# Adding the residual inside the PSUM accumulator and computing the closing norm at the tile seam, in a one-core hybrid encoder step

## The reference

```
q     = (rmsnorm(x2) * norm_ffn) @ w_q          # 8 heads, two halves of 128
s1,s2 = q1 @ keys1.T, q2 @ keys2.T              # 128 scores each
eidx, g = top 16 of the 16 x 16 best pairs, softmax over them
u     = peer_u[eidx];  act = gelu(u . xn)       # 8 * 16 = 128 experts a token
out   = sum over experts of g * act * peer_v[eidx]
y     = rmsnorm(x2 + out) * norm_final
```

## Time and profile before

| | |
|---|---|
| median of 3 runs | 3584.15 us (3577.04 to 3598.55) |
| the profiled execution | 3598.55 us, span from first to last instruction 3596.6 us |
| busy share of the span | TensorE matmuls 89%, DVE 68%, ACT 39%, GpSimd 39% |
| moved | 1336.42 MB, 372 GB/s over the span |
| mean granted TensorE clock | 0.962 of full |

### The profile page before, as it was taken

One profiled execution on the slowest core, in us unless ns is written; L12 is line 12 of the kernel. 1 busy time (PEld: TensorE's weight loads), 2 busy tenths in 40 slices (PEclk: granted clock), 3 DMA queues, 4 the chain that ended last, 5 costly groups with the idle time before them and its releaser, 6 DMA issues.

```text
span 3596.6 us, 33769 instructions
## 1 busy us (share of the span) xinstructions
PE 3197.2 (89%) x10016; PEld 1828.4 (51%) x10016; DVE 2433.1 (68%) x5507; ACT 1409.6 (39%) x4197; POOL 1401.1 (39%) x1240
## 2 busy tenths in 40 slices
PE   7888999999999998999999998999999877777776
PEld 6676555555555555555655555555655322322232
DVE  6633579777656689777656588777666666666674
ACT  4312444554333344554333444554333333333332
POOL 1101445333343444333333344434333444454443
PEclk9899998999999998999999998999999999999999
DMA  4257998999999998999999997999999999999998
GB/s 135 72 169 239 380 418 334 367 419 379 419 405 417 410 405 321 376 410 389 419 405 404 404 407 291 389 409 400 419 409 405 409 420 420 394 420 414 414 403 348
DMA packets 232071, 1336.42 MB, mean 372 GB/s; under 512 B 27664, under 2 KB 49296, under 8 KB 92624
## 3 DMA queue, kind: packets, MB, share of 16 engines
q0 software_dynamic: 156672, 1140.92, 78.0%
q1 hardware_dynamic: 62992, 179.96, 13.7%
q10 hardware_dynamic: 12224, 13.38, 1.0%
HBM read 1310.93 MB, written 23.23 MB: 371 GB/s over the span
## 4 chain that ended last, share of the span: by engine, by line
PE 61%; DMA 20%; ACT 8%; DVE 5%; issue 5%; POOL 1%; POOLq 0%; SPq 0%; DVEq 0%; ACTq 0%
PE ps_acc L757 33%; DMA rows<-in_experts,idx 19%; PE ps_a L593 15%; PE ps_v L593 5%; PE ps_a L668 3%; DVE rows L1363 2%; ACT uy L814 2%; POOL rows L1509 1%; PE ps_y L635 1%; ACT coef L908 1%; ACT diag L912 1%; PE ps_a L695 1%; DVE va L1208 1%; ACT L905 1%; PE ps_a L672 1%
## 5 line engine op out<-in xcount | busy, mean ns | idle before, releaser
L757 PE MATMUL ps_acc<-rows,diag 128*128 128x512 f32 x4352 | 2052.8, 620 | 319.8 <-ACT diag L912 316.6
L1509 POOL DMA_INDIRECT rows<-in_experts,idx x1088 | 1272.5, 1170 | 1878.4 <-PE ps_acc L757 1516.9
L1363 DVE CUSTOM_DVE_ANT_0 rows<-rows,xn 128x1024 f32<-128x1024 f32 x1088 | 1331.1, 1233 | 845.8 <-DMA rows<-in_experts,idx 832.4
L757 PEld LDWEIGHTS ps_acc<-rows,diag 128*128 128x128 f32 x4352 | 839.9, 198 | 1370.3 <-issue 862.7
L905 ACT ACTIVATE act_v<-dots 128x2 f32<-128x2 f32 x544 | 109.8, 202 | 1170.0 <-DVE dots L1363 1158.2
L912 ACT ACTIVATE diag<-pk,coef 128x128 f32<-128x128 f32 x1088 | 377.2, 394 | 17.7
L593 PE MATMUL ps_a<-xnT,ring 128*128 128x272 f32 x1536 | 375.1, 400 | 0.9 <-ACT xnT L802 0.7
L593 PEld LDWEIGHTS ps_a<-xnT,ring 128*128 128x128 f32 x1536 | 297.5, 194 | 93.1 <-issue 35.0
L908 ACT ACTIVATE coef<-act_v,soft 128x1 f32<-128x1 f32 x1088 | 261.4, 287 | 17.8
L593 PE MATMUL ps_a<-gates,ring 128*128 128x272 f32 x1024 | 247.7, 395 | 4.2 <-issue 3.4
L1208 DVE SCALAR_TENSOR_TENSOR va<-va,pk 128x302 f32<-128x302 f32 x480 | 247.1, 579 | 1.9
(11 more groups left out here) (224 smaller groups left out, 2240.6 us busy)
## 6 DMA issues: line engine op xcount, KB each, us to landing
ring<-in_slabs SPq DMA_DIRECT2D x256, 512.0 KB
rows<-in_experts,idx POOLq DMA_INDIRECT x1088
ring<-made_slabs SPq DMA_DIRECT2D x24, 512.0 KB
sc<-score_rows SPq DMA_DIRECT2D x68, 128.0 KB
score_rows<-gp ACTq DMA_DIRECT2D x32, 256.0 KB
xt<-in_x_prompt SPq DMA_DIRECT2D x4, 1024.0 KB
x_rows<-xt ACTq DMA_DIRECT2D x4, 1024.0 KB, 11.6
x2t<-x_rows SPq DMA_DIRECT2D x8, 512.0 KB
```

The costliest lines, as they stand in the source:

```text
L757: ins = pe.matmul(ps_acc[:, h, :], diag[:, slot, :], rows[:, slot, D + h * 512:D + (h + 1) * 512], start=first, stop=False, skip_group_che ...
L1363: ins = dve.tensor_tensor_reduce(rows[:, slot, 0:D], rows[:, slot, 0:D], xn[:, :], 1.0, 0.0, ALU.mult, ALU.add, dots[:, s:s + 1])
L1509: pool.indirect_dma_start(out=rows[:, slot, :], out_offset=None, in_=experts, in_offset=bass.IndirectOffsetOnAxis(ap=idx[:, a, k:k + 1], a ...
```

## The change

The old sum of accumulator and residual on DVE goes. Instead TensorE opens each tile's accumulation itself: `start(t)` multiplies the identity with the tile's `x2t` rows and writes `ps_acc` with `start=True`; all slots then accumulate onto it. The closing norm reads `ps_acc` directly: ACT squares it, DVE takes the mean, ACT takes the square root, DVE takes the reciprocal and scales out of PSUM into `yt`. All of that now stands at the first turn of the next tile, on ACT ahead of the batches of the new tile, on DVE after its first four dots, and the store too. TensorE waits for the scaling (`y_ready`) before it opens the next tile. GpSimd has no part in it any more. `x2t` has one buffer; it is loaded when TensorE has opened and DVE has normed the tile before, for odd tiles at the second turn of the group instead of the fourth.

```
-        x2t = sb("x2t", [P, 2, D])
+        x2t = sb("x2t", [P, D])
...
             def rows_free(t):
-                if t >= 2:
-                    sp.wait_ge(y_sq, t - 1)
-                    pass_wait()
+                sp.wait_ge(acc_begun, t + 1)
+                pass_wait()
+                sp.wait_ge(xn_ready, t + 1)
+                pass_wait()
...
-                if k == 3 and g < GROUPS:
+                if k == 1 and g < GROUPS:
                     load_rows(2 * g + 1)
-                if k == 1 and g < GROUPS:
                     sp.wait_ge(score_out[1], 128 * g + 64)
...
-                if turn > 32 and turn % 32 == 3:
-                    store(turn // 32 - 1)
+                if ended_at(turn) is not None:
+                    store(ended_at(turn))
...
+            def start(t):
+
+                w = DEC if t == TILES else P
+                pe.wait_ge(x2_in, loads_of(t))
+                pe.wait_ge(y_ready, t + 1)
+                for h in range(2):
+                    last = pe.matmul(ps_acc[:, h, :], eye[0:w, :], x2t[0:w, h * 512:(h + 1) * 512],
+                                     start=True, stop=False, skip_group_check=True)
+                last.then_inc(acc_begun, 1)
+
             def slots(n, s0, s1):
                 for s in range(s0, s1):
-                    slot, first = s % RING, s == 0 and n % TPAIRS == 0
-                    if first and n:
-                        pe.wait_ge(y_sum, n // TPAIRS)
+                    slot = s % RING
                     pe.wait_ge(diag_done, PAIR * n + s + 1)
...
-                                        start=first, stop=False, skip_group_check=True)
+                                        start=False, stop=False, skip_group_check=True)
...
                 if turn % 32 == 0:
                     beside(2 * turn + 1)
+                    start(turn // 32)
                     slots(n, s, s + STEPS)
...
             def end_squares(t):
-                act.wait_ge(y_sum, t + 1)
-                act.activation(x2t[:, t % 2, :], yt[:, :], ACT.Square, accum_out=fin[:, 0:1]).then_inc(y_sq, 1)
+
+                steps = PAIR * (TILES * TPAIRS + SPAIRS) if t == TILES else PAIR * TPAIRS * (t + 1)
+                act.wait_ge(y_out, 16 * t + 16)
+                act.wait_ge(slot_free, RING + steps)
+                act.activation(yt[:, :], flat(ps_acc[:, :, :]), ACT.Square, accum_out=fin[:, 0:1]).then_inc(y_sq, 1)
+
+            def end_root(t):
+                act.wait_ge(y_ms, 1 * t + 1)
+                act.activation(fin[:, 2:3], fin[:, 1:2], ACT.Sqrt).then_inc(y_std, 1)
...
                 if turn % 32 == 0:
+                    if t is not None:
+                        end_squares(t)
                     beside(2 * turn)
+                    if t is not None:
+                        end_root(t)
                     pair_start(n, r)
                     batch(n, TB * r)
...
                 batch(n, TB * r + 1)
-                if t is not None:
-                    end_squares(t)
                 beside(2 * turn + 1)
...
             def end(t):
-                steps = PAIR * (TILES * TPAIRS + SPAIRS) if t == TILES else PAIR * TPAIRS * (t + 1)
-                dve.wait_ge(y_out, 16 * t + 16)
-                dve.wait_ge(slot_free, RING + steps)
-                dve.tensor_tensor(yt[:, :], flat(ps_acc[:, :, :]), x2t[:, t % 2, :], ALU.add).then_inc(y_sum, 1)
-
-            def end_mean(t):
-
-                dve.wait_ge(y_sq, t + 1)
+                dve.wait_ge(y_sq, 1 * t + 1)
                 dve.tensor_scalar(fin[:, 1:2], fin[:, 0:1], 1.0 / D, EPS, ALU.mult, ALU.add).then_inc(y_ms, 1)
-
-            def end_scale(t):
-
-                dve.wait_ge(y_std, t + 1)
-                dve.scalar_tensor_tensor(yt[:, :], yt[:, :], fin[:, 2:3], gl[:, :], ALU.mult, ALU.mult).then_inc(y_ready, 1)
+                dve.wait_ge(y_std, 1 * t + 1)
+                step(dve.reciprocal(fin[:, 3:4], fin[:, 2:3]))
+                dve.scalar_tensor_tensor(yt[:, :], flat(ps_acc[:, :, :]), fin[:, 3:4],
+                                         gl[:, :], ALU.mult, ALU.mult).then_inc(y_ready, 1)
...
-            def end_root(t):
-
-                pool.wait_ge(y_ms, t + 1)
-                pool.tensor_tensor(fin[:, 2:3], fin[:, 1:2], half[:, 0:1], ALU.pow).then_inc(y_std, 1)
```

More of the change, by code:

```diff
@@ L334, in program @@
         sp_passed = sem("sp_passed")
-        y_sum = sem("y_sum")
+        acc_begun = sem("acc_begun")
         idx_ready = sem("idx_ready")
@@ L451, in rows_free @@
             def rows_free(t):
-                if t >= 2:
-                    sp.wait_ge(y_sq, t - 1)
-                    pass_wait()
+                sp.wait_ge(acc_begun, t + 1)
+                pass_wait()
+                sp.wait_ge(xn_ready, t + 1)
+                pass_wait()
             def load_rows(t):
                 rows_free(t)
-                sp.dma_start(x2t[:, t % 2, :], x2_t[t]).then_inc(x2_in, 16)
+                sp.dma_start(x2t[:, :], x2_t[t]).then_inc(x2_in, 16)
                 sp.dma_start(rst[:, t % 2, :], rs_t[t]).then_inc(rs_in, 16)
@@ L532, in _ @@
                         half_tile = slice(f * DEC, (f + 1) * DEC)
-                        sp.dma_start(x2t[half_tile, TILES % 2, :], x2_d[SEQ:SEQ + DEC, :]).then_inc(x2_in, 16)
+                        sp.dma_start(x2t[half_tile, :], x2_d[SEQ:SEQ + DEC, :]).then_inc(x2_in, 16)
                         sp.dma_start(rst[half_tile, TILES % 2, :], rs_d[SEQ:SEQ + DEC, :]).then_inc(rs_in, 16)
@@ L767, in _ @@
             pe.sem_inc(slot_free, RING)
+            pe.sem_inc(acc_begun, 1)
             pe.sem_inc(y_done, 2)
@@ L969, in _ @@
                 batch(n, TB * r + 1)
-                if t is not None:
-                    end_squares(t)
                 beside(2 * turn + 1)
             end_squares(TILES)
+            end_root(TILES)
         @block.vector
@@ L1376, in start @@
                 dve.wait_ge(rs_in, loads_of(t))
-                dve.scalar_tensor_tensor(xn[:, :], x2t[:, t % 2, :], rst[:, t % 2, 0:1], gf[:, :], ALU.mult, ALU.mult).then_inc(xn_ready, 1)
+                dve.scalar_tensor_tensor(xn[:, :], x2t[:, :], rst[:, t % 2, 0:1], gf[:, :], ALU.mult, ALU.mult).then_inc(xn_ready, 1)
                 dve.wait_ge(xn_ready, 1 * t + 2)
@@ L1433, in _ @@
                         choose(n + 1, r)
[L1434 to L1437, removed]
             end(TILES)
-            end_mean(TILES)
-            end_scale(TILES)
         @block.gpsimd
@@ L1536, in _ @@
                         ahead(n, r, b)
-                if turn > 32 and turn % 32 == 1:
-                    end_root(turn // 32 - 1)
-            end_root(TILES)
 def _lay_out(inputs):
```

## The result

The changed kernel took 3599.3 us in the median of 7 runs (3591.29 to 3606.69), the kernel before 3575.73 in 7 runs beside it: a ratio of 1.0055, interval 1.0029 to 1.0082, so some 20 us more (10 to 29). A second set of runs of the same two kernels gave 1.0045 (1.0027 to 1.0063), 16 us. Both intervals lie above 1, so it is slower, by about the half per cent that the prediction took as the limit of "the same". The time is inside the range; the loss is about three times the predicted +6. That 3599.3 falls even within the forecast's own 3580 to 3600 is luck: the prediction counted from a median of 3584.15 over three runs of the kernel before, and on the 3575.73 of seven runs its +6 would have given 3582. The profiled execution took 3593.31 us (span 3591.5).

A forecast was written before the change was run, and what follows sets the result against it. DMA, over 90% busy and mostly with expert-row gathers, was taken as the bound. Four starving seams (6.4 us), four covered ones (0) and the tail (-0.3) gave +6 us, 3590 on the 3584.15 median; range 3570 to 3612.

The forecast's parts named there:

- Restart of TensorE: At each tile start, TensorE restarts at D + 2.1 instead of D + 1.27, 0.8 us later; D ends the fourth dot.
- starving starts: Tile starts where the DMA engines run idle; four predicted, each losing 2.8 us less 1.2 for the store.
- covered starts: Tile starts where DMA share stays at 1.01 or more, near 771, 1158, 1573 and 2383 us; four predicted.
- Seed: Four TensorE instructions of the identity matmuls ahead of slot 0: 2.0 us, between 1.75 at full clock and 3.5.
- Both together: Later TensorE restart plus seed: gathers restart 0.8 + 2.0 = 2.8 us later at each seam, bounds 2.5 and 4.3.
- Table loads: Two ACT loads of 1.28 us per seam, for Sqrt and back to Gelu, hidden behind other work at no cost.
- rival 3: Sqrt's table load is exposed on ACT but the covered seams' slack holds: +12 to 15 us, 3598; chance 0.20.
- The store's 1.2 back: The 512 KB store, moved into the seam, fills idle DMA: each starving seam gets 1.2 us back.
- Covered starts cost 0: At seams where DMA stays full, slack of 2.85 us, 4.1 with the store queued, absorbs the delay: cost 0.
- the signs that the prediction named: Wrong if covered seams show idle DMA, Sqrt's load starts after the mean, Square comes after D, or a slab is late.
- Sum: Four starving seams x (2.8 - 1.2) = 6.4, four covered ones 0, tail -0.3: +6 us over the kernel before.
- rival 1: Every seam pays in full, covered ones having no slack: 22 to 33 us more, 3606 to 3617; chance 0.26.

The follow-up runs named there:

- seed_only: Kernel before, with only the start of the sum by identity matmuls added and DVE copying where it added; norm unmoved: 3593.19 us, ratio 1.0047.
- pow_at_seam: Changed kernel with root and reciprocal done as one power on GpSimd, so no Sqrt or table loads at the starts: 3596.25 us, ratio 1.0049.
- late_store: Changed kernel with the finished tile's store issued at its old place, three turns into the new tile: 3600.11 us, ratio 1.0055.
- dead_covered: Kernel before, with four dead 128x512 matmuls ahead of slot 0 of tiles 1, 3 and 5 only: ratio 1.0024, 9 us more.
- before_end_early: Kernel before, with DVE's add of the tile put behind the second of the new tile's four dots: 3574.55 us, ratio 0.9996.

## Why the prediction came out as it did

*Restart of TensorE (+0.8).* Right at the five starving starts: D + 2.05 in the profile after. Wrong in its path at 1, 3 and 5: there the fourth dot isn't the last wait, the Square behind the old tile's last matmul is. "ACT's Square needs only the last matmul of the old tile, so it is done" holds only where the rows land late. At the covered starts Square, load, Sqrt and scaling make 4.2 us behind that matmul where the kernel before had its add hidden under layer work. That the restart is 0.9 later there as well (4.4 us behind the last matmul, against 3.5) is luck.

*Seed (2.0 of bounds 1.75 to 3.5).* Four instructions took 3.75 us at tile 7 and 1.96 at tile 3. Net, by seed_only, the gather came 1.7 later at each (at tile 3, gap 7.91 against 6.19). Right there, but too small as a mean of the starving starts, where it was 2.7.

*Both together (2.8, bounds 2.5 to 4.3).* 2.7 at the covered starts, 3.3 at tile 7, 4.1 at tile 8 (D + 10.3 against D + 6.2). From the old tile's last matmul on, the five starving starts average (72.4 - 53.3) / 5 = 3.8; 3.5 of it lies behind D, and 0.3 is a later fourth dot. Within the bounds, but the term was sized low.

*Table loads.* At starving starts hidden, as predicted. At covered ones the load for Sqrt is exposed (rival 3's mechanism), at a small price by pow_at_seam. The trace has 254 loads on ACT against 240, 14 more where I expected 16. At tile 3 the load begins 0.03 behind the work ahead of it, and Sqrt at 1566.68, 0.01 behind the end of the load. The Trainium skill (ScalarE: Activation LUTs, What ACT_TABLE_LOAD costs) counts a drain of 1.38 us with each load; this trace has none. The prediction's estimate by that figure should also have been 4 x 0.8 = 3.2 us, not 4.

*The store's 1.2 back.* Idle time at the starts does fall by 5.7 us in all with the early store, not in the time. At the covered starts, where the prediction let the store raise the slack from 2.85 to 4.1, it had the wrong sign: some 3 us more idle in the odd tiles with the store at the seam than without (late_store).

*Covered starts cost 0.* This is the step that failed. I read "DMA share 1.02 right behind that seam" as slack and priced how late one gather could be. But a full DMA share behind a start says only that the queue isn't empty yet. In the changed kernel the windows at these starts stay full indeed, and each covered start loses about 2 us more than before by D + 78, 17 against 11 for the three; the odd tiles lose 8 us more. TensorE makes up nothing on the way: its start behind the hold-up moves from D + 38.9 to D + 41.6 (means of six), by the 2.7 of the restart. Late_store puts about half of that down to the delay of 2.7 and half to the store, taken from ahead of the hold-up. Two of the signs that the prediction named were there in part: at tile 3 Square ends 0.3 after the fourth dot, though no work of the layer plan stands ahead of it, and Sqrt's load begins with the mean (1565.39 against 1565.40), not before it.

*Sum.* +6 was four starving starts of 1.6 each. In the second profile of the kernel before, the start of tile 2 loses 2.5 us too, which had none in the first, so there are five. Measured idle DMA is up by 8 us in the odd tiles, where the sum had 0, and by 6 in tiles 6 to 8, where it had three times 1.6. By rival 1's account (eight delays of 2.8, 22 us, the store back at some) the measured 16 to 20 is nearly met, and rival 1 had only 0.26. Its time is met better than its mechanism, as the covered starts do have some slack and part of their loss is the store's. Over all kernels in the table the time follows the gap: 7 to 10 us of gap cost 9 or 10 us, 18 to 28 cost 13 to 20, 34 cost 26. Reasoning from the DMA side was right, the place where slack was assumed was not. What stays open: in seed_only 17 us stand against 9 of idle time found in tiles 1, 3, 5 to 8, with the rest in the even tiles' spread or in slower transfer; why dead_covered costs 9 us with 4 to 5 of idle time; and why 16 us less gap in before_end_early gave nothing measurable, beyond the 4 us of idle time that it won in tiles 6 to 8.

## What to carry to other kernels

A full DMA share right behind a stall isn't slack if the kernel has another stall within one ring of backlog or a few: follow the queue to the next place where it runs dry, and price the delay there. A transfer that is moved leaves a hole where it was: look whether it stood ahead of such a place. When work is put on the path between the last use of an accumulator and its first reuse, look for the starts at which the old partner of that path was hidden under other work, and count from the last event of each start, which need not be the same everywhere. A delay of known size put in alone, dead matmuls ahead of the restart, prices such slack, if it is made as long as the change's own delay and not longer.

## What the runs showed of the hardware

TensorE after 6.65 us without work ran the seed's four 128x512 instructions in 3.75 us at a granted clock of 0.50 (1.2 GHz), after 0.72 us without work in 1.96 at a granted clock of 1.00. ACT's table loads took 1283 ns each, all of them. One with a single wait ahead of its activation ran before the wait was over (3082.37, where Sqrt itself began at 3085.92), one with two waits ahead only after them (341.70 in the earlier trace rows); the instruction behind a load began 0.01 us after its end. One kernel's times spread over up to 35 us in 12 runs. In the two traces of the kernel before, tile 2 took 414.6 and 407.3 us and tile 4 422.6 and 411.0, while tiles 6, 7 and 8 took 335.5, 332.6, 173.7 and 334.2, 331.3, 174.1. What makes the difference in tiles 2 and 4 wasn't found.
